# A PEER gather ring that runs on over stage boundaries, with 16 tokens left over to the next mixing stage

## What is computed

```python
q = jnp.einsum('td,de->te', xb, w_q)...            # scores -> 128 experts per token (idx), gates
act = jax.nn.gelu(jnp.einsum('thkd,td->thk', u_tab[idx], xb))
return jnp.einsum('thk,thkd->td', gate * act, v_tab[idx])   # then layer norm of alpha*x + this -> y
```

## Time and profile before

| | us |
|---|---|
| runs of the kernel before | 5026.23, 5030.12, 5057.6 |
| median | 5030.12 |
| the profiled execution: span, first to last instruction | 5061.9 |

### The profile page before, as it was taken

How to read it: one execution, slowest core, us unless ns; L and a number is a source line. 1 busy time by engine, 2 the same in 40 slices (tenths; PEclk the granted TensorE clock), 3 DMA queues, 4 the chain that set the end, 5 groups by cost and what they waited for, 6 DMA issues and landing times. The chain is left out here.

```text
span 5061.9 us, 53189 instructions
## 1 busy us (share of the span) xinstructions
PE 3427.8 (68%) x17745; PEld 1968.4 (39%) x17745; DVE 3195.1 (63%) x7030; ACT 725.4 (14%) x2596; POOL 2650.2 (52%) x2240
## 2 busy tenths in 40 slices
PE   7978377599887576556579988757656564565516
PEld 5666262255462452343144446245234322321101
DVE  5335896588544896677668744489667755664370
ACT  2141110111210210210022121021021011000000
POOL 1000376465435575676546533557567647726564
PEclk9988668699888678776789999877877776677659
DMA  5453478899859789989879875978999988879897
GB/s 180 145 192 119 175 262 327 295 368 353 322 181 366 268 314 369 336 320 335 336 271 355 307 293 167 369 275 307 368 344 321 367 317 300 303 295 361 300 370 281
DMA packets 460478, 1497.56 MB, mean 296 GB/s; under 512 B 53184, under 2 KB 115456, under 8 KB 447632
## 3 DMA queue, kind: packets, MB, share of 16 engines
q0 software_dynamic: 317952, 1141.01, 61.7%
q1 hardware_dynamic: 121040, 330.55, 17.6%
q10 hardware_dynamic: 21216, 22.60, 1.4%
HBM read 1455.22 MB, written 55.52 MB: 298 GB/s over the span
## 5 line engine op out<-in xcount | busy, mean ns | idle before, releaser
L2122 POOL DMA_INDIRECT e_ring<-peer_u,e_idx x1024 | 1325.0, 1294 | 647.9 <-issue 231.6
L2122 POOL DMA_INDIRECT e_ring<-peer_v,e_idxT x1024 | 1119.7, 1093 | 891.4 <-PE e_ff L2274 445.5
L2158 DVE CUSTOM_DVE_ANT_0 e_ring<-e_ring,e_x 128x1024 f32<-128x1024 f32 x1024 | 1226.5, 1234 | 291.1 <-DMA e_ring<-peer_u,e_idx 270.6
L2274 PE MATMUL e_ff<-e_ring,e_strips 128*32 128x512 f32 x4096 | 672.4, 786 | 512.0 <-DMA e_ring<-peer_v,e_idxT 429.5
L352 PE MATMUL p_ps<-p_hT,p_w 128*128 128x256 f32 (+2 forms) x1728 | 569.9, 484 | 0.0
L2274 PEld LDWEIGHTS e_ff<-e_ring,e_strips 128*32 128x32 f32 x4096 | 146.5, 129 | 933.9 <-issue 931.7
L352 PEld LDWEIGHTS p_ps<-p_hT,p_w 128*128 128x128 f32 x1728 | 329.0, 195 | 209.0 <-issue 129.5
L1138 POOL CAST hidden<-delta 128x128 bf16<-128x128 f32 (+1 forms) x9 | 2.9, 317 | 629.7 <-DMA delta<-hidden 605.7
L376 PE MATMUL p_ps<-p_w,p_hT 128*128 128x512 f32 (+1 forms) x576 | 251.2, 599 | 0.0
L1299 PE MATMUL bank<-X,atp 128*128 128x128 f32 (+1 forms) x1120 | 170.5, 304 | 102.3 <-DVE XT L1736 70.7
L1313 PE MATMUL bank<-T,XT 128*128 128x128 f32 (+1 forms) x1088 | 167.8, 304 | 93.1 <-DVE T L1744 91.4
(11 more groups left out here) (392 smaller groups left out, 5150.1 us busy)
## 6 DMA issues: line engine op xcount, KB each, us to landing
p_w<-w_in SPq DMA_DIRECT2D x156, 512.0 KB, 3.6
wbuf<-wc SPq DMA_DIRECT2D x56, 1024.0 KB
wbuf<-w_out SPq DMA_DIRECT2D x40, 1024.0 KB
e_ring<-peer_v,e_idxT POOLq DMA_INDIRECT x1104
atp<-w_out SPq DMA_DIRECT2D x16, 1024.0 KB
kb_kdec<-w_out SPq DMA_DIRECT2D x16, 1024.0 KB
atp<-wc SPq DMA_DIRECT2D x16, 1024.0 KB
e_ring<-peer_u,e_idx POOLq DMA_INDIRECT x1024
```

What stands on the lines that cost most here:

```text
L2122: g.indirect_dma_start(out=self.ring[:, i % RING, :], out_offset=None, in_=table[:, :], in_offset=at, bounds_check=NEXP - 1, oob_is_err=Fa ...
L2158: v.tensor_tensor_reduce(out=self.ring[0:U, i, :], in0=self.ring[0:U, i, :], in1=self.x[0:U, :], scale=1.0, scalar=0.0, op0=ALU.mult, op1= ...
L2274: last = nc.tensor.matmul(self.ff[i][32 * j:32 * j + 32, :], self.strips[:, self.strip_of[t] % NSTRIP, j, 31 - s:63 - s], self.ring[:, sel ...
```

## The change

1. The ring is never renumbered. A `Plan` per stage, all made ahead, carries the slot offset (`base`) and the landings so far (`counts`) from stage to stage. The landing semaphores are left out of the clearing at a stage's end; one more barrier clears them at the very end.
2. `pool_end` no longer waits for the landings, signals `gathered` or resets the rings. Instead it issues the first gathers of the next stage, up to 12. Tail tokens, and head tokens of a stage without u rows, have known indices (`known`); u rows of the next tile (up to `fresh`) wait until its choice is copied (`taken`). Each waits for its slot. mix 0 has no ring of its own and issues the first 12 u rows of mix 1 at its end. The folded stage gets none ahead.
3. Tile 1's last 16 tokens go from mix 2 to mix 3 as its tail, and tile 2's head in mix 3 goes down from 80 to 64 and its tail in mix 4 up from 48 to 64. The same is done with tiles 4 and 5 in mix 5, 6 and 7.
4. A mixing stage's tail has a share of 14 (of 78.4) at `start`, and a projecting stage's tail has 4 after each tile's layer norm.
5. ACT computes the exponential of the choice ahead of its last checkpoint, not behind it.
6. The diff also has branches for u rows split over stages and for an early turn (`early`). With these plans none is taken.

```diff
 def project_points(tiles):
-    w = {"ln": (2, 2, 0)}
+    w = {}
+    for i in range(len(tiles)):
+        w["ln", i] = (4, 0, 0)
+    w["ln"] = (0, 2, 0)
...
-    "series": {"start": (0, 0, 0), "norm": (0, 0, 0), ...
+    "series": {"start": (14, 0, 0), "norm": (0, 0, 0), ...
...
 class Plan:
+    def slot(self, g):
+        return (self.base + g) % RING
+    def known(self):
+        n = 0
+        while n < min(RING, len(self.seq)) and (self.seq[n][0] == "v" and (self.seq[n][1] < self.n_tail or not self.U) or
+                                                self.seq[n][0] == "u" and not self.starts):
+            n += 1
+        return n
+    def fresh(self):
+        n = self.known()
+        while n < min(RING, len(self.seq)) and self.seq[n][0] == "u":
+            n += 1
+        return n
...
     def pool_end(self, g):
+        S, p, then = self.S, self.plan, self.then
         self.pool_at()
-        for i in range(RING):
-            if self.landings[i]:
-                g.wait_ge(S[f"in{i}"], 16 * self.landings[i])
-        g.sem_inc(S["gathered"], 1)
-        nums = [S[f"in{i}"].num for i in range(RING)]
-        g.dma_reset(range(min(nums), max(nums) + 1))
+        if then is None:
+            return
+        for i in range(then.fresh()):
+            if i == then.known():
+                g.wait_ge(S["taken"], 4)
+            if len(p.seq) + i >= RING:
+                self.freed(g, len(p.seq) + i - RING)
+            self.gather(g, S, then, i)
...
     def take_choice(self, v):
-        v.wait_ge(S["gathered"], 1)
         self.copy_choice(v, S)
         v.wait_ge(S["taken"], 4)
...
 # mix_tile, ACT
-                for e in range(EH):
+                for e in range(EH - 1):
                     at("best", e)
                 act.wait_ge(S["soft"], 1)
                 nc.scalar.activation(B["best"][0:R], B["best"][0:R], ACT.Exp).then_inc(S["exp_ready"], 1)
+                at("best", EH - 1)
                 peer.scalar_end(act)
...
 # program
+        stages = [
+            (1, dict(u=(0, 0, SLOTS), head=(0, 0, 80))),
+            ([2, 3, 4], dict(tail=(0, 80, P), u=(1, 0, SLOTS))),
+            (2, dict(head=(1, 0, 112))),
+            (3, dict(tail=(1, 112, P), u=(2, 0, SLOTS), head=(2, 0, 64))),
+            (4, dict(tail=(2, 64, P), u=(3, 0, SLOTS), head=(3, 0, 64))),
+            ([5, 6, 7, LAST], dict(tail=(3, 64, P), u=(4, 0, SLOTS))),
+            (5, dict(head=(4, 0, 112))),
+            (6, dict(tail=(4, 112, P), u=(5, 0, SLOTS), head=(5, 0, 64))),
+            (7, dict(tail=(5, 64, P), u=(6, 0, SLOTS), head=(6, 0, 64))),
+            (LAST, dict(tail=(6, 64, P), u=(7, 0, SLOTS), head=(7, 0, P)))]
```

More of the change, by code:

```diff
@@ L288, in _ @@
                 ident = B["ident"]
-                if peer:
+                if peer and peer.plan.starts:
                     peer.tensor_start(pe, ps[5])
@@ L679, with __init__ @@
     names = ["k_keys", "k_wq0", "k_wq1", "k_wq2", "k_comb", "k_evac", "k_wc0", "k_wc1", "k_clear", "taken"]
[L681 to L684, removed]
+    def __init__(self, io, e, then):
+        self.io, self.e, self.then, self.plan = io, e, then, Plan(checkpoint_weights("rows"), u=(0, 0, SLOTS))
+        self.upto = dict(self.plan.upto)
+        self.plan.starts = self.plan.turns = self.plan.early = False
     def begin(self, nc, ctx, S):
-        self.nc, self.S, self.U = nc, S, 0
+        self.nc, self.S = nc, S
     def steps(self, emit):
@@ L714, in pool_end @@
         g.wait_ge(self.S["k_clear"], 1)
+        g.wait_ge(self.S["taken"], 4)
+        for i in range(self.then.fresh()):
+            self.e.gather(g, self.S, self.then, i)
     def tensor(self, pe):
@@ L1481, in _ @@
                 at("turn")
-                if peer.U:
+                if peer.plan.turns and not peer.plan.early:
                     peer.tensor_turn(pe, bank[3])
@@ L1498, in _ @@
                     if half == 0:
-                        if i == 1 and peer.U:
+                        if i == 1 and peer.plan.turns and not peer.plan.early:
                             pe.wait_ge(S["w_taken"], 1)
@@ L2497, in experts_folded @@
         nc.all_engine_barrier(sems_to_clear=S.range)
+        nums = [x.num for x in pool_dma.values()]
+        nc.all_engine_barrier(sems_to_clear=range(min(nums), max(nums) + 1))
 def store_states(nc, io, B):
@@ new lines, in program @@
+        plans, base, counts = [], 0, [0] * RING
+        for some, parts in stages:
+            mixed = None if isinstance(some, list) else some
+            points = project_points(some) if mixed is None else checkpoint_weights("series" if "u" in parts else "tokens")
+            plans.append(Plan(points, base, counts, mixed=mixed, **parts))
+            plans[-1].sent = plans[-1].fresh()
+            base, counts = base + len(plans[-1].seq), plans[-1].counts
+        project(nc, io, B, [0, 1], pool_dma, consts=Constants(io, B, e))
@@ L2542, in program @@
+        e.bind(io, B, None, None)
+        mix_tile(nc, io, B, pool_dma, 0, Keys(io, e, plans[0]))
+        for (some, _), plan, then in zip(stages, plans, plans[1:] + [None]):
+            e.bind(io, B, plan, then)
+            if plan.mixed is None:
+                project(nc, io, B, some, pool_dma, peer=e)
+            else:
+                mix_tile(nc, io, B, pool_dma, plan.mixed, e)
+        experts_folded(nc, e, pool_dma, base, counts)
         store_states(nc, io, B)
```

277 lines of the change are left out of this document (142 added, 135 removed).

## The result

The changed kernel takes 5149.7 us (median of 4 runs, 5131.3 to 5176.5) beside 5029.5 us for the kernel before on the same chip (4 runs, 5026.2 to 5057.6). The ratio is 1.0228, 95% interval 1.0185 to 1.027: slower by 2.3%, and outside the predicted range of 4945 to 5080.

What follows compares the result with a forecast made beforehand. No single engine was taken as the bound: it changes by stage and within stages, and DMA runs dry at boundaries. A +58, B -18, C -42, D -16 and last barrier +2 gave -16: 5014 us, range 4945 to 5080.

Steps and rivals of the forecast that it cites:

- Part A: Stage ends: POOL issues up to 12 more gathers ahead of the barrier, so next stages start later; +58 us.
- about 1.5 from the last engine's end to SP's first load: At each stage's end, the time charged between POOL's last issue ending and the next stage's first load.
- the 0 for project 2-4: End of project 2-4: stage ends on PE and POOL is done by then, so gathers ahead add 0.
- Part B: Stage starts: u rows already landed save waiting, net -4 in each of six mixing stages; -18 us, between -39 and +40.
- The contention that I charged: Stage starts: loads run beside the tail of the gathers; 2.5 us charged, +3 in each projecting stage.
- Part C: Tokens moved between stages, to stage starts and into the layer norm, with normalize moved mid-stage; -42 us.
- half of the slope: First half of mix 3 and 6: 12 tail tokens inside, 14.4 us each at full slope; +14 taken, range 0 to +29.
- The half step and the normalization: Mix 3 and 6 get a mid-stage normalize, 6.4 us of DVE where DVE is nearly full; +13, at best 0.
- Part D: Later u-row waits in mix 1, 3 and 6 (about 4 us) and mix 2 and 5 (2 us) shrink; -16, 0 to -35.
- The one that ended on the other side: Stage starts: head start paid at barrier and next loads, tokens cost the same anywhere; +87, 5117 us; chance 0.20 to 0.17 listed as slower 0.17.
- The one by which the idle DMA time comes back whole: Stage boundaries: transfers bound these stretches, so 79 us of idle DMA time is gained; -119, 4911 us; chance 0.20.

Runs made afterwards that it cites:

- the one chip: The unaltered changed kernel and the kernel before, both run again on one chip of the follow-up runs: 5048.8 us, ratio 1.0231, and 4948.9 us.

## Why the prediction was wrong, point by point

**Part A failed, in two steps.** The first is "about 1.5 from the last engine's end to SP's first load". I took that number from boundaries where PE or DVE came last and POOL had waited for its own landings, and used it for a POOL that comes last with twelve transfers under way. The rest of that step was right. In mix 0 it is 16.4 us from the choice (555.4) to the end of the twelfth issue (571.8), where I had 15.6; with 1.5 behind them mix 0 would have been 15.2 us longer, against 15.7 forecast and 20.4 measured (322.1 for 301.7 us). At the end of mix 3, POOL's issues alone would have ended the stage at 2121.3, 8.7 us behind PE's 2112.6 (2111.2 + 1.4), where I forecast 6.8; the drain made it 18.3. The second failed step is the 0 for project 2-4: its last u rows are freed by DVE only just ahead of the end, so its twelve gathers ahead are all under way there. Together with the 2.8 us of project 5-8 the drain cost 81 us: some 44 for landings after the last issue, 34 for what the drain took behind the last packet, and the 2.8.

**Part B** came in half of the stages. L1743 stands 16.4 us after the start of mix 3, not 22.1, 14.9 in mix 6 (22.5) and 15.3 in mix 1 (21.8), more than the 4 us forecast. In mix 4, 7 and 8, where twelve tail tokens come first, it stands at 21.7, 21.9 and 21.7 us, against 20.6, 21.5 and 22.5: the 4 us forecast for each did not come. The wait for the gates was 4.4 to 6.0 us in the six (4.5 to 6.5 before), so the loads did not meet the gathers. They could not, since the drain had kept them apart. L1828, L1912 and L1743 in mix 3 and 4, against the earlier trace rows:

```profile
L1828 DVE TENSOR_TENSOR r_tmp<-rows x1: 1226/1226/1226, 1914.2 to 1914.2; 128x1024 f32<-128x1024 f32 x1
L1828 DVE TENSOR_TENSOR r_tmp<-rows x1: 1221/1221/1221, 2368.8 to 2368.8; 128x1024 f32<-128x1024 f32 x1
L1912 DVE SCALAR_TENSOR_TENSOR h<-h,bank x2: 680/681/682, 2000.3 to 2000.9; 128x512 f32<-128x512 f32 x2
L1912 DVE SCALAR_TENSOR_TENSOR h<-h,bank x2: 680/681/682, 2463.9 to 2464.5; 128x512 f32<-128x512 f32 x2
L1743 DVE TENSOR_TENSOR atp<-bank,dec x16: 414/416/425, 1742.0 to 1829.7; 128x256 f32<-128x256 f32 x16
L1743 DVE TENSOR_TENSOR atp<-bank,dec x16: 414/416/425, 2152.5 to 2273.9; 128x256 f32<-128x256 f32 x16
```

The contention that I charged is real where the drain is gone: 9.4 us for the gates instead of 4.7. The Trainium skill ("DMA: Bandwidth & Descriptors", Queues, rings and completion order) has each DMA engine take turns between its queues; the trace without the drain agrees in kind, its gates coming 4.7 us later in mix 4. That is more than the 1.9 us I had worked out from that rule, but those were for 3.7 us of transfers left, and here gathers are still being issued beside the loads.

**Part C** had the right signs, and its terms were too favourable. In mix 3 the phase from L1743 to L1828 grew from 160.3 to 172.2 us, +11.9, and in mix 6 from 157.4 to 171.7, +14.3. I had +14 for the two together, half of the slope; the whole slope, 14.4 each, was nearer. The half step and the normalization took +5.5 from L1828 to L1912 in mix 3 (+6.5 forecast). On the one chip, mix 3 up to its choice took 372.8 us against 386.7, and mix 6 375.5 against 387.2. But there the kernel before waited 5.6 and 4.3 us for `gathered` ahead of the choice; without these waits it is -8.3 and -7.4, where parts B to D had -16. The half behind L1912 gave 18 us in each, not 21.5. Mix 4 took 418.1 against 413.4. With its wait of 1.7 us taken off in the same way that is 6.4 us more, for a forecast of +0.8 from B and C.

Mix 2 came to its choice only 1.7 us sooner (319.6 for 321.4) and mix 5 5.9 us, where the closing `normalize` and the tokens should have given some 15 each. From L1912 to the choice they did win 9.4 and 10.2 us, the half that DVE bounds. Ahead of it 7.7 and 4.3 us were lost again. On the chip of the result the same two stretches differ by +0.9 and -0.6 us, so this loss may be no more than the difference between two executions; there mix 2 and 5 came to their choice 7.3 and 8.1 us sooner, still half of the forecast. No run tells why. On the one chip this is the largest part of the 29 us that the drain does not cover.

**Part D** failed. The row in the changed kernel:

```profile
DVE e_ring L2215 <- DMA e_ring<-peer_u,e_idx: 19.0, 14, 8.1
```

DVE waits 19.0 us for u rows against 17.5. The 8.6 us at the start went, and an 8.1 us wait came further on. POOL still stands at the mask cast until 1735.3 in mix 3, so the ring is not refilled any sooner. The 8.1 us wait stands at 1908.8, 183 us into the stage, where eight rows sent ahead can no longer help. No run tells what made it.

**The rivals.** The one that ended on the other side was near in time (5117 for 5150) and had "paid at the barrier and again at the next loads" right for the first half; its mechanism was contention at the starts, and that is not what happened in the changed kernel; it is what happens once the drain is gone (gates 4.1 to 6.0 us later). The one by which the idle DMA time comes back whole is refuted by the runs without the drain. There the 30 us around the end of mix 3 show no pause at all,

```profile
2050.00:2080.00 30.00, 12.35 (x77) 2.68 (x69) 11.55 (x26) 1.88 (x7) 14.61 (x15) 0.78 1.02 405
```

against a share of 0.82 in the kernel before:

```profile
2030.00:2060.00 30.00, 14.37 (x91) 7.99 (x93) 5.39 (x11) 9.39 (x29) 9.47 (x11) 0.77 0.82 314
```

and the kernel is still no faster than before. In windows of 30 us around ten boundaries, the DMA engines' idle time adds up to 105 us in the kernel before, 41 in this run and 50 in the one with known gathers alone (the pauses at the starts of mix 1, 3 and 6 stay). That one stands at 0.9989: with 55 us of the pauses filled, the work is done 0.1% sooner, 0.2% at most. The idle time at the boundaries was not what bounded this kernel.

**The sum.** On the experiments' chips, in shares of the time before: the changed kernel is +2.3%. The drain is 1.6 of that. With it gone, the old split and no u rows behind the choice take off another 0.8, nearly all of it the u rows. What is then left, known gathers ahead, the start shares and the running ring, is -0.1%, nothing that a measurement tells from 0.

## What to carry to other kernels

Here a barrier that drained GpSimd also waited for the DMAs that it had sent, so work sent ahead over the barrier was finished at the barrier, not behind it. Before sending ahead, look at which waits the old code had just ahead of the barrier: if it waited for its own landings, the short barrier in its trace says nothing about one with transfers under way. And where every engine is idle and the DMA share is 1, the head start is being paid in full. The view of busy time does not show such a wait; a query of the block's line does, where the `DRAIN` has its duration.

## What was not expected of the hardware

GpSimd's drain waited until the gathers had landed: 9 us with DMA at 1.02 and all engines idle. It went on for another 0.4 to 5.1 us without any transfer, nearly the same time for the same number of gathers in the stage; the reason is open. Without the drain, a barrier of semaphores let the next stage start with seven of twelve gathers not yet issued; the engine's queue runs over the barrier. A lone gather of 512 KB held the drain only about 2.7 us beyond its issue. And gathers issued every 1.30 us fill the DMA engines exactly (a share of 1.02 to 1.04).
